# Choosing the first eight row numbers of a router head from 64 sums instead of 256

## What is computed

```python
def peer(h, wq, subkeys, u_tab, v_tab):
    q = (hf @ wq).reshape(T, PEER_HEADS, 2, PEER_DKEY // 2)
    sc = jnp.einsum('thpd,pnd->thpn', q, subkeys, preferred_element_type=jnp.float32)
    top_v, top_i = lax.top_k(sc, PEER_TOPK)
    cand_v = (top_v[:, :, 0, :, None] + top_v[:, :, 1, None, :]).reshape(T, PEER_HEADS, -1)
    cand_id = (top_i[:, :, 0, :, None] * PEER_NKEYS + top_i[:, :, 1, None, :]).reshape(T, PEER_HEADS, -1)
    best_v, best_j = lax.top_k(cand_v, PEER_TOPK)
    ids = jnp.take_along_axis(cand_id, best_j, axis=-1)
    gates = jax.nn.softmax(best_v, axis=-1)
    ...
    # per block of 128 rows: a = x . u_tab[ids], w = gates * gelu(a), y = sum w * v_tab[ids]
```

## Time and profile before

| what | value |
|---|---|
| median of 3 runs | 1242.38 us (1241.58 to 1244.21) |
| span of the profiled execution | 1229.3 us |
| first head's first row numbers ready (last instruction starts) | 208.94 us |
| first gather issued | 210.10 us |
| first product on a gathered row | 217.66 us |
| POOL held before the `v` gather of slot 4 | 9.81 us, until 241.19 us |

### The profile page before, as it was taken

The page is one execution under the profiler, slowest core; times in us unless marked ns, Lnnn a source line. Parts: engine busy times, 40 slices in busy tenths (PEclk is TensorE's granted clock), DMA queues, the critical chain, the costliest instruction groups (busy, mean ns, idle before and its releaser), DMA issues.

```text
span 1229.3 us, 11227 instructions
## 1 busy us (share of the span) xinstructions
PE 1009.4 (82%) x3303; PEld 544.6 (44%) x3303; DVE 638.0 (52%) x1482; ACT 274.1 (22%) x741; POOL 534.5 (43%) x589
## 2 busy tenths in 40 slices
PE   4999999799888519767867857777579999999998
PEld 4768557554443204323323323323224645566454
DVE  6447676684754339636737646664443324311532
ACT  4022322112211102111105111110111253313540
POOL 1300003566666757667657667575766001200100
PEclk9999999899989859979779868887778999999999
DMA  9997765899999989989999989898989736333300
GB/s 346 308 371 253 277 212 163 318 366 336 356 365 362 413 340 357 373 334 400 347 353 398 350 347 408 325 413 335 412 342 364 269 137 206 95 111 137 137 1 34
DMA packets 123697, 361.75 MB, mean 294 GB/s; under 512 B 13464, under 2 KB 20256, under 8 KB 123520
## 3 DMA queue, kind: packets, MB, share of 16 engines
q0 software_dynamic: 76000, 276.39, 59.3%
q1 hardware_dynamic: 45008, 82.97, 19.1%
q10 hardware_dynamic: 2640, 1.81, 0.5%
HBM read 360.08 MB, written 1.05 MB: 294 GB/s over the span
## 4 chain that ended last, share of the span: by engine, by line
PE 74%; issue 14%; DVE 5%; another core or an unknown queue 3%; DMA 2%; ACT 2%; POOL 0%; DVEq 0%; POOLq 0%; ACTq 0%
PE bank L1492 36%; PE bank L1536 13%; PE bank L1256 9%; PE bank L1305 2%; PE bank L1246 2%; PE bank L1237 2%; DVE R L1784 1%; PE bank L1574 1%; PE bank L1346 1%; DMA small<-in_c 1%; PE bank L1322 1%; PE bank L1438 1%; PE bank L1417 1%; PE bank L1269 1%
## 5 line engine op out<-in xcount | busy, mean ns | idle before, releaser
L1492 PE MATMUL bank<-wring,R 128*128 128x512 f32 x496 | 238.9, 628 | 54.6 <-issue 53.0
L2040 DVE CUSTOM_DVE_ANT_0 wring<-wring,bank 128x1024 f32<-128x1024 f32 x160 | 194.2, 1218 | 150.2 <-DMA wring<-in_peer_u,ids 108.7
L769 POOL DMA_INDIRECT wring<-in_peer_v,ids x160 | 152.2, 951 | 125.4 <-issue 61.2
L1492 PEld LDWEIGHTS bank<-wring,R 128*128 128x128 f32 x496 | 98.2, 200 | 191.4 <-issue 186.8
L769 POOL DMA_INDIRECT wring<-in_peer_u,ids x160 | 152.9, 956 | 52.0 <-issue 44.2
L1536 PE MATMUL bank<-wring,hT 128*128 128x512 f32 (+1 forms) x384 | 167.4, 588 | 3.0 <-ACT R L1187 2.5
L1492 PE MATMUL bank<-R,modb 128*128 128x512 f32 x192 | 93.8, 635 | 58.3 <-ACT modb L998 38.2
L808 POOL TENSOR_SCALAR small<-small 128x2 f32<-128x2 f32 (+3 forms) x16 | 3.1, 194 | 304.4 <-ACTq L865 160.7
L1536 PEld LDWEIGHTS bank<-wring,hT 128*128 128x128 f32 x384 | 71.1, 190 | 83.8 <-issue 79.6
L1492 PE MATMUL bank<-hT,modb 128*128 128x512 f32 x96 | 63.2, 758 | 50.9 <-issue 49.1
L1492 PEld LDWEIGHTS bank<-R,modb 128*128 128x128 f32 x192 | 38.7, 203 | 111.6 <-issue 72.6
(11 more groups left out here) (292 smaller groups left out, 1326.4 us busy)
## 6 DMA issues: line engine op xcount, KB each, us to landing
wring<-in_w_in SPq DMA_DIRECT2D x12, 2048.0 KB, 12.1
wring<-in_ada_w SPq DMA_DIRECT2D x8, 2048.0 KB, 13.5
wring<-in_w_out SPq DMA_DIRECT2D x6, 2048.0 KB, 10.4
wring<-in_ada_w SPq DMA_DIRECT2D x8, 1024.0 KB, 14.7
wring<-in_peer_wq SPq DMA_DIRECT2D x2, 2048.0 KB, 7.9
wring<-in_w_in SPq DMA_DIRECT2D x4, 1024.0 KB, 10.6
wring<-in_w_in SPq DMA_DIRECT2D x2, 1792.0 KB, 12.6
wring<-in_peer_u,ids POOLq DMA_INDIRECT x160
```

Of the source, the lines that this page charges most:

```text
L769: pool.indirect_dma_start(dst, None, table, bass.IndirectOffsetOnAxis(index, 0)).then_inc(landed, 16)
L1492: last = pe.matmul(pb[half][:, :], diag[b][:, s, :], v_place(n, b, s)[:, half * 512:(half + 1) * 512], start=False, stop=closing and s == ...
L2040: dve.tensor_tensor_reduce(row, row, h_psum(t), 1.0, 0.0, ALU.mult, ALU.add, a8[:, b, s:s + 1]).then_inc(u_free, 1)
```

## The change

The first head's choice is written anew. ACT writes the two halves' scores of the first head of `("s0", 0)` straight to `one_piece`, so the copy of part 0 goes away. `first_eight` takes the top eight of each half (parts 1 and 2), forms the 64 sums of them in a spare tile, takes the top eight of these, finds their indices by a shift of 3 and a mask of 7, compares with eight numbers of `iota` instead of sixteen, and signals `first_head_ready`. `other_eight` then does what was left out: parts 3 to 5, a strike-out of the eight found among the 64, a copy of the 64 into the 16 by 16 square, the other 192 sums by two additions, and then parts 10 and 11 and 12 to 16 as before.

```diff
-                    free(act.activation(scores[:, 0, 2 * h:2 * h + 2, :].rearrange("p a b -> p (a b)"), pb[:, 0:2 * P], ACT.Copy),
-                         ("s0", h))
+                    halves_of_head = one_piece[:, 0:2, :] if h == 0 else scores[:, 0, 2:4, :]
+                    free(act.activation(halves_of_head.rearrange("p a b -> p (a b)"), pb[:, 0:2 * P], ACT.Copy), ("s0", h))
...
-            for part in range(9):
-                choose(0, part, 0, 1)
-            for part in range(12, 17):
-                choose(0, part, 0, 1, 0, GROUP)
-            for part in range(9, 12):
-                choose(0, part, 0, 1)
-            for part in range(12, 17):
-                choose(0, part, 0, 1, GROUP, TOPK)
+            def first_eight():
+                sums, values, found = cand[:, 1, 0:GROUP * GROUP], best_v[:, 0, 0:GROUP], best_j[:, 0, 0:GROUP]
+                parts = best_ab[:, 0, :, 0:GROUP]
+                hits = region(9216, 2, GROUP, GROUP)
+                square = [P, 2, GROUP, GROUP]
+                for part in (1, 2):
+                    choose(0, part, 0, 1)
+                chain.wait()
+                chain.link(dve.tensor_tensor(sums.rearrange("p (a b) -> p a b", a=GROUP),
+                                             bc(top_v[:, 0, 0, 0:GROUP].unsqueeze(2), GROUP, GROUP),
+                                             bc(top_v[:, 0, 1, 0:GROUP].unsqueeze(1), GROUP, GROUP), ALU.add))
+                chain.link(dve.max(values, sums))
+                chain.link(dve.max_index(found, values, sums))
+                chain.step(dve.tensor_scalar(parts[:, 0, :], found, 3, None, ALU.logical_shift_right))
+                chain.step(dve.tensor_scalar(parts[:, 1, :], found, 7, None, ALU.bitwise_and))
...
+                dve.sem_inc(first_head_ready, 1)
+
+            def other_eight():
...
+                for part in (3, 4, 5):
+                    choose(0, part, 0, 1)
+                chain.step(dve.match_replace(sums, best_v[:, 0, 0:GROUP], sums, -3.0e38))
+                chain.wait()
+                chain.step(dve.tensor_copy(corner[:, 0:GROUP, 0:GROUP], sums.rearrange("p (a b) -> p a b", a=GROUP)))
+                chain.step(dve.tensor_tensor(corner[:, 0:GROUP, GROUP:TOPK], bc(v0[:, 0:GROUP].unsqueeze(2), GROUP, GROUP),
+                                             bc(v1[:, GROUP:TOPK].unsqueeze(1), GROUP, GROUP), ALU.add))
+                chain.step(dve.tensor_tensor(corner[:, GROUP:TOPK, :], bc(v0[:, GROUP:TOPK].unsqueeze(2), GROUP, TOPK),
+                                             bc(v1.unsqueeze(1), GROUP, TOPK), ALU.add))
+                for part in (10, 11):
+                    choose(0, part, 0, 1)
+                for part in range(12, 17):
+                    choose(0, part, 0, 1, GROUP, TOPK)
```

More of the change, by code:

```diff
@@ L2011, in _ @@
             drained(dve, ("s0", 0))
-            for part in range(9):
-                choose(0, part, 0, 1)
-            for part in range(12, 17):
-                choose(0, part, 0, 1, 0, GROUP)
-            for part in range(9, 12):
-                choose(0, part, 0, 1)
-            for part in range(12, 17):
-                choose(0, part, 0, 1, GROUP, TOPK)
+            def first_eight():
[13 more added lines that the diff above has]
+                chain.step(dve.tensor_scalar(parts[:, 1, :], found, 7, None, ALU.bitwise_and))
+                chain.link(dve.tensor_tensor(shifted[:, 0:1, 0:GROUP], best_v[:, 0:1, 0:GROUP], bc(best_v[:, 0:1, 0:1], 1, GROUP),
+                                             ALU.subtract))
+                chain.link(dve.tensor_tensor(hits, bc(parts.unsqueeze(3), 2, GROUP, GROUP),
+                                             iota[:, 0:GROUP].unsqueeze(1).unsqueeze(1).to_broadcast(square), ALU.is_equal))
+                chain.link(dve.tensor_tensor(hits, hits, bc(top_i[:, 0, :, 0:GROUP].unsqueeze(2), 2, GROUP, GROUP), ALU.mult))
+                chain.link(dve.tensor_reduce(picked[:, 0, :, 0:GROUP], hits, AX.X, ALU.add))
+                chain.link(dve.scalar_tensor_tensor(ids[:, 0:GROUP].rearrange("p (h k) -> p h k", h=1), picked[:, 0:1, 0, 0:GROUP],
+                                                    float(NKEY), picked[:, 0:1, 1, 0:GROUP], ALU.mult, ALU.add))
+                dve.sem_inc(first_head_ready, 1)
@@ new lines, in other_eight @@
+            def other_eight():
+                sums, corner = cand[:, 1, 0:GROUP * GROUP], cand[:, 0, :].rearrange("p (a b) -> p a b", a=TOPK)
+                v0, v1 = top_v[:, 0, 0, :], top_v[:, 0, 1, :]
+                for part in (3, 4, 5):
[11 more added lines that the diff above has]
+                    choose(0, part, 0, 1, GROUP, TOPK)
@@ L2020, in _ @@
+            first_eight()
+            other_eight()
             dve.memset(zeros, 0.0).then_inc(zeros_set, 1)
```

## The result

Before: 1241.78 us, median of 6 runs (1236.18 to 1244.21). Changed: 1232.49 us, median of 6 runs (1231.96 to 1233.05). The ratio is 0.994, 95% interval 0.9922 to 0.9958: a gain of 5 to 10 us. The forecast was 1242.0 with a range down to 1238.6. A later comparison of the same two kernels gave 1232.01 and 1226.17 us, ratio 0.9944 (0.9928 to 0.9961). So the gain is alike, while the level is not: the four later comparisons have the kernel before at 1231.6 to 1232.8 us, and why the first one had it at 1241.8 is not shown.

What follows compares the result with a forecast made beforehand. PE held 74% of the last-ending chain, and the change paid only where PE or transfers wait for DVE. The path's sum was 0, less 0.4 us for PE's crawl: 1242.38 - 0.4 = 1242.0 us, 8-in-10 range 1238.6 to 1245.6.

Steps and rivals of the forecast that it cites:

- the first eight row numbers: DVE's first-head choice: 3.2 us shorter, write ending at 205.9 us, first gather at about 206.9 us.
- the first data: First gathered rows: held behind POOL's own loads on the same queue, so the first product gains only 0 to 0.3 us.
- Rival A: First gathers: rows land up to 3 us sooner, the burst ends 3.2 us sooner; 1239.2 us, chance 0.20.
- the 9th gather: POOL's burst: it reuses slot 0, so must wait for the first product until about 219.1 us; 1.3 us lead left.
- DVE's second half: `other_eight` on DVE: roughly 0.4 us net saved, between 0 and 1, hidden by a 4.44 us wait for rows.
- Second, POOL's burst ends at a fence that DVE's choice does not move: After 17 gathers POOL waits 9.81 us for PE's queries at L1256; sooner gathers only lengthen that pause.
- the sum on the path: Whole kernel: 0 us, since PE's queries start from untouched data and order from 241.19 us on is the same.
- the term for the slow stretch: PE's crawl, 223.1 to 234.2 us: ends 1.3 us sooner with POOL's burst, or unmoved with the bytes; 0.4 us taken.
- rival B: PE's crawl starts up to 3.2 us sooner but ends with the bytes: 3.9 us slower, 1246.3 us, chance 0.18.
- PE slow before 221 us: Sign on PE's queries that would show the forecast wrong and rival B right.
- About 13.1 us of the median lie outside the span: Base of the sum: span of 1229.3 us, with the median 13.1 us above it.

Runs made afterwards that it cites:

- the repeat: The changed kernel run again unchanged: 1226.17 us beside 1232.01 for the kernel before, ratio 0.9944; for the slow stretch, the kernel before run again, ratio 0.9998.
- loads later: Changed kernel with POOL's eight own loads for the second block moved behind the first piece: ratio 0.9977 to the kernel before.
- v rows first: Changed kernel with the first four v gathers issued ahead of the second group's u gathers of these slots: 1224.42 us beside 1232.78 of before, ratio 0.9924.
- the repeat of before: The kernel before, run again unchanged: ratio 0.9998, with POOL resuming at 240.87 us.
- half rows: The kernel before with gathers of 2 KB instead of 4 KB per row, sums not computed rightly: one run, 1231.42 beside 1232.01 us.
- the slower POOL: The kernel before with a memset of one column ahead of every gather: 1231.7 us, ratio 0.9995.
- two products waited for: The kernel before with the 9th and 11th gathers waiting for the second product instead of the first and second: ratio 0.9976.

## Why the prediction was wrong

**Right: the first eight row numbers.** Predicted 3.2 us sooner, ending at 205.9 and the first gather at 206.9; measured 205.66 + 0.17 = 205.83 and 206.83. The three 64-wide operations took 0.22, 0.23 and 0.22 us where the slope gives 0.22, 0.23 and 0.22, and the 128-wide compare 0.29 as the slope gives: down to 64 elements there is no floor.

**Right in the main: the first data.** Predicted a first product at 217.3 to 217.7; measured 217.97, and 219.97 us in the repeat, which is why the break was longer there. It came no sooner than before, as forecast. The loads ahead on the queue held it, as the kernel with the loads moved back showed. The Trainium skill (DMA: Bandwidth & Descriptors, Queues, rings and completion order) says that a DMA engine takes turns between the queue rows that have work for it. The traces agree that what stands ahead in the same row holds up a gather: the first product came 5.45 us after its gather without these loads, 11.14 us with them. Rival A, early rows, did not happen, and where it was made to happen (loads later) it gave less than the changed kernel.

**Right: the 9th gather.** Predicted to wait until about 219.1; measured 219.99, after 3.36 us idle. DVE's second half was hidden under 6.09 us of waiting.

**Wrong: what the break is worth.** The prediction booked this wait only as the loss of a lead: "only about 1.3 us is left from the ninth gather on". It was the source of the gain. The step that failed is "Second, POOL's burst ends at a fence that DVE's choice does not move". PE's end at that fence moved from 240.38 to 231.16 us, and POOL's resumption by 7.37 us, where the sum on the path had 0 and the term for the slow stretch 0.4 us. The prediction had the slow stretch in view and asked when it ends (with POOL's last issue or with the bytes), at most 1.3 us. It did not ask what starts it, and so not whether a break inside the burst would keep it from starting. Two rows that hint at the answer were there: the slow stretch begins only after 223.68 - 210.10 = 13.6 us of gathers 1.24 us apart, and in the 8.5 us before it the DMA engines are just as full. Costed from those, a break after 8 gathers could have given the 6 queries of the slow stretch and the 17 at the lower clock back: 23 queries in 23 x 0.22 = 5.1 us instead of 240.38 - 223.68 = 16.7, so up to 11.6 us, against the 9.2 measured.

**Partly right: rival B's mechanism.** PE did stumble sooner, at 215.5 to 217.65 us, while POOL's first eight gathers went out. In 2.15 us it did 4 of them instead of some 10. By the prediction's own sign ("PE slow before 221 us") this is case B, with a forecast of 1246.3 us; the kernel became faster all the same. For the end of the slow running did not stay with the bytes: steady running began 1.0 us after POOL's eighth issue ended (216.63).

**What is left of the 9.2 us.** POOL resumed 7.4 and not 9.2 us sooner. It waits for PE's last query itself, not for ACT. Where PE ended long after POOL's burst, POOL went on 0.8 us after PE (240.38 to 241.19 in the kernel before). Here PE ended at 231.16 and POOL went on at 233.82, 2.66 us after PE and 2.96 us after its own last issue (229.93 + 0.93 = 230.86). In the repeat and with v rows first it was 2.79 and 2.88 us after the last issue. So POOL's own wait seems to be noticed late behind its burst, as the slow stretch of PE outlasts the burst; why is not shown.

ACT's copy of the queries at 233.04 looks like the same delay, but most of it has a plain reason. ACT works in program order, and ahead of the copy stands an exponential (L986) that waits for DVE's softmax shift (L1981), written at 231.62 + 0.17 = 231.79 us:

```profile
231.62 0.17 DVE L1981 TENSOR_TENSOR R<-R 128x16 f32<-128x16 f32 x1
```

```profile
224.28 0.60 ACT L1012 ACTIVATE R<-bank 128x512 f32<-128x512 f32 x1 [5.08 <-PE bank L1256]
231.97 0.23 ACT L986 ACTIVATE R<-R 128x32 f32<-128x32 f32 x1 [7.09 <-issue]
233.04 0.60 ACT L1012 ACTIVATE R<-bank 128x512 f32<-128x512 f32 x1 [0.85 <-remote]
```

**Wrong: the base of the sum.** "About 13.1 us of the median lie outside the span" was the median less the span of one execution. Measured with both numbers of one execution, 1232.45 for a span of 1230.7, it is 1.8 us. The profiled execution of before was about 11 us quicker than the median beside it. Since the sum went from the median and the two ends cancel, this did not move the forecast, but it made the profile seem more typical than it was. Whether the stretches that it shows were also there in the slower executions isn't known from one trace; the repeat shows that the slow stretch is.

**Open.** The break's worth at the fence (5 to 8 us) and the whole gain do not go one to one: with equal resumptions near 236 us the ratios run from 0.9944 to 0.9995. Part of the lead is lost again later: in the five traces that resume at 240.3 to 241.8 us the last gather follows 706.9 to 710.7 us after the 18th, in the nine that resume at 232.7 to 236.7 us 708.9 to 718.7 us. In single executions the time from the 18th to the last gather differs by up to 11 us, for instance:

```profile
952.47 0.94 POOL L769 DMA_INDIRECT wring<-in_peer_v,ids  x1 [0.30 <-issue]
```

in the changed kernel (718.7 us after its 18th), and in its repeat

```profile
947.17 0.94 POOL L769 DMA_INDIRECT wring<-in_peer_v,ids  x1 [0.30 <-issue]
```

(711.5 us). What in POOL's issuing slows the others (its instruction work, its semaphore traffic, or the descriptors) was not separated. It is shown only that the bytes and packets do not, and that a break does help. Why the slow stretch sets in sooner when the gathers begin sooner is open as well.

## What to carry to other kernels

When an engine's row breaks up into single instructions with "issue" gaps while another engine issues gathers back to back, ask what starts the slow stretch, and try a break of about 2 us in the gathers before shortening anything. A wait that a change adds can be a gain if it stands inside such a burst and the engine that is slowed holds the next fence. It paid here only where that fence was the next thing late: breaks in all later groups gave no gain that could be measured. And take the part outside the span from one execution's own time, not from a median.

## What the runs showed that was not expected

- PE's queries, 0.22 us each, came 0.7, 1.4 or 2.1 us apart during a long burst of gathers; around 600 us its matmuls came 2.8 us apart. The granted clock was 1.00 ahead of it (2.4 GHz) and 0.72 to 0.76 on the mean over the stretch with the single instructions; in the kernel before it stood at 0.50 (1.2 GHz) from 229 to 237 us, and the 17 queries behind the stretch took 0.40 us each.
- The slow stretch ended soon after POOL's last issue: 2.15 us after it before (231.38 to 233.53), 2.88 us at the next halt (273.18 to 276.06), 1.8 us in the repeat of before, 2.0 us with half rows, 0.6 us with the slower POOL.
- PE's finished work is seen late during a burst: with two products waited for, the queries ended at 229.58 us. ACT, free for their copy from 233.26 us, began it at 235.85, 2.6 us later; POOL, done with its burst at 234.51, went on at 236.62, 2.1 us later.
- Gathers of 2 KB rows instead of 4 KB rows took POOL as long to issue (0.94 us), and the one run took about the time of the kernel before.
